# A streaming encoder layer on one core: a VectorE copy, one idle product, later loads of the mix's weights, and unequal last parts

## The chip, the cores and the metric

The kernel runs on one core of one Trainium2 chip. The metric is the device time of one execution in microseconds (us).

## The reference, cut to what matters

One layer works on 2176 tokens (2048 of a prompt, and 8 streams with 16 tokens each) of 1024 features. A projection feeds two groups of heads: a gated unit whose rows are mixed over 128 tokens by a triangular matrix, and a band attention. The two halves go through an output projection, and a layer norm closes.

```python
h = jnp.einsum('bsd,de->bse', x, w_in)
v_a = _layernorm(jax.nn.gelu(h[..., o[1]:o[2]]), ln_v_g, ln_v_b)
mix = jnp.einsum('gts,bnsgc->bntgc', jnp.tril(w_s), vc) + b_s.T[...]      # a = u * mix
y = jnp.concatenate([a_out * silu(z_a), b_out * silu(z_b)], axis=-1)
out = jnp.einsum('bse,ed->bsd', y, w_out)
return _layernorm(ALPHA * x + out, g, bb)
```

For the streams the mix uses the first 16 rows and columns of `w_s` only.

## The kernel before, in words

Every large product is done in three products of a shortened format: each operand is split into a high part (ScalarE copies it into that format) and a low part (VectorE subtracts the high part from the original), and TensorE adds high x high, high x low and low x high. Work is written out by hand for five engines, each with its own list of instructions in program order; semaphores tie them together. SP's list holds most DMAs, ScalarE's list the loads of weights.

**The opening.** The 2176 tokens are 17 tiles of 128. The first stage ("va") projects each tile on 512 columns, v_a's. Its weights come as 8 pieces (`wp`, order `KO`), and each tile's transposed x comes as two halves of 4 blocks. ScalarE asks for the 8 pieces (L1143 to L1148), then turns piece 0, the first half of tiles 0 and 1, pieces 1 and 2, the second halves of tiles 0 and 1, and the other pieces into high parts (L1149 to L1158), each counted in `w_high` or `xt_high`. VectorE makes the low parts in the same order (L1480 to L1490, counted in `w_ready` and `xt_ready`). TensorE first runs `IDLE_PRODUCTS` products of a tile of ones that nobody reads (L1882 to L1884), then takes tiles 0 and 1 together, piece by piece: high of tile 0, high of tile 1, two products with the weights' low part, two with x's low part (L1886 to L1903). The first product of the fifth piece counts in `xt_freed`, which lets SP reload tile 0's first half for tile 2.

From tile 2 on (L1904) TensorE goes: first half of tile t, the mix of tile t - 2, second half of tile t. The mix of tile 0 waits for `const_ready` at 6 (L1831), which is the two masks that GpSimd puts on the mix's weights: `wt` for the prompt and `wts`, the eight 16 x 16 blocks for the streams (L940 to L943). It begins with products that sum the rows of `wt`. Behind the masks in GpSimd's list stands, for each tile, the sum that turns a tile's mean and variance into a scale and a shift (L988 to L997); ScalarE then normalises the tile (L1102) and only then turns the second half of tile t + 2 (L1170 to L1180). The mix of tile 1 waits for its offsets `mix_b`, which VectorE makes once, in tile 1's turn, behind the low part of tile 3's second half (L1523 to L1531), from the row sums, `b_sgu` (`bs`) and the columns `v_cols`.

**SP's list in the opening** (L741 to L756): the four halves of tiles 0 and 1; `bs`; `v_cols`; `wt`; eight loads of blocks into `wts` behind the wait for `zeroed` (GpSimd's clearing of it); `rel_in`, the table of relative biases; then for each tile t the two halves of tile t + 2, each behind the wait that its buffer is free (`load_xt`, L631 to L639), and at t = 1, 4, 7, 10 four loads of x for the next stage.

**The end.** The last stage projects each tile's 1024 output columns in two halves. For the last four tiles VectorE does the layer norm by itself (`finish`, L1697 to L1710): subtract the mean and multiply by the gain, in two parts of 512 columns, wait for GpSimd's inverse deviation, multiply by it and add the offset, in two parts again. SP stores tiles 15 and 16 part by part (L912 to L916).

```python
            for t in range(TILES):
                for h in range(2):
                    if t + 2 < TILES:
                        load_xt("va", t + 2, h)
                    if h == 0 and t in X_LOADS:
                        load_xo(X_LOADS.index(t))
```

Of the kernel before, what the change touches and what calls it, by code (L numbers as in the profile page):

```python
# [6 lines left out]
P = 128  # L7
D = 1024
KC = D // P
HK = KC // 2  # L10
# [3 lines left out]
TILES = T // P  # L14
# [14 lines left out]
MASKED = 3.0e38  # L29
KR = 6  # L30
TAIL = 4
IDLE_PRODUCTS = 10

# [21 lines left out]
KO = [0, 1, 2, 3, 4, 5, 7, 6]  # L57
# [124 lines left out]
BUILT = builds()  # L182
# [42 lines left out]
XT_ORDER = [("va", 0, 0), ("va", 1, 0), ("va", 0, 1), ("va", 1, 1)]  # L225
XT_ORDER += [(*e, h) for e in XT_TILES[2:] for h in range(2)]
XT_COUNT = {half: n + 1 for n, half in enumerate(XT_ORDER)}


def xt_place(kind, t, h):  # L230

    if (kind, t) == ("v", TILES - 1):
        return 6 + h
    if t % 2:
        return 2 + h
    return 4 + h if kind == "v" and t > V_SPLIT else h


def xt_signal(kind, t):

    return 2 if (kind, t) == ("v", TILES - 1) else t % 2
# [44 lines left out]
V_CYCLES = TILES - V_EARLY  # L286
CYCLES = V_CYCLES + 2 * TILES
START = [V_CYCLES + 2 * n for n in range(TILES)]
STORE = [START[n] + (3 if n < TILES - TAIL else 2) for n in range(TILES)]
X_LOAD = [V_CYCLES, V_CYCLES] + [STORE[n - 2] for n in range(2, TILES)]  # L290
POOL_TILES = TILES - TAIL
# [40 lines left out]
def hybrid_stream_step(nc, x, x_t, x_tiles, w_tok, w_pair, w_o, w_sgu, b_sgu, ln_v_g, ln_v_b, ln_v_cols, rel_rev, ln_g, ln_b,  # L332
# [6 lines left out]
    with ctx:  # L339
# [3 lines left out]
        def sem(name):  # L343
            return ctx.enter_context(nc.semaphore(name))
# [13 lines left out]
        def at(name, offset, shape, dt=f32):  # L358
# [10 lines left out]
        lnvg, lnvb, bs, wt, wts = (at(name, x_slot * j + 8 * HK * WIDTH[0], shape) for j, (name, shape) in enumerate((  # L369
            ("lnvg", [512]), ("lnvb", [512]), ("bs", [GRP, P]), ("wt", [GRP, P]), ("wts", [GRP, P]))))  # L370
# [31 lines left out]
        xt_h = [at(f"xt_h{b}", a, [HK, P], f32r) for b, a in enumerate(xt_at)]  # L402
        xt_l = [at(f"xt_l{b}", a + 2048, [HK, P], f32r) for b, a in enumerate(xt_at)]
        xt_f = [at(f"xt_f{b}", a + 2048, [HK, P]) for b, a in enumerate(xt_at)]
# [9 lines left out]
        v_cols = at("v_cols", here + 224, [2 * GRP])  # L414
# [64 lines left out]
        cols_loaded = sem("cols_loaded")  # L479
# [10 lines left out]
        xt_loaded = [[sem(f"xt_loaded{b}_{h}") for h in range(2)] for b in range(3)]  # L490
        q_part = sem("q_part")
        q_copied = sem("q_copied")
        xt_high = sem("xt_high")
        xt_ready = sem("xt_ready")
        xt_freed = sem("xt_freed")
# [134 lines left out]
        def _(sp):  # L630
# [109 lines left out]

            for t, h in ((0, 0), (1, 0), (0, 1), (1, 1)):  # L741
                load_xt("va", t, h)
            sp.dma_start(bs[:].rearrange("p g t -> p (g t)"), b_sgu.partition_broadcast(P)).then_inc(cols_loaded, 16)
            sp.dma_start(v_cols[:], ln_v_cols).then_inc(cols_loaded, 16)
            sp.dma_start(wt[:], w_sgu).then_inc(par_loaded, 16)
            sp.wait_ge(zeroed, 1)
            for b in range(SB):
                sp.dma_start(wts[b * SN:(b + 1) * SN, :, b * SN:(b + 1) * SN],
                             w_sgu[0:SN, :, 0:SN]).then_inc(blocks_loaded, 16)
            sp.dma_start(rel_in[0:HEADS, :], rel_rev).then_inc(rel_loaded, 16)  # L750
            for t in range(TILES):
                for h in range(2):
                    if t + 2 < TILES:
                        load_xt("va", t + 2, h)
                    if h == 0 and t in X_LOADS:
                        load_xo(X_LOADS.index(t))  # L756
                if t == 4:
                    sp.wait_ge(rel_shifted, 2)
                    sp.wait_ge(rel_filled, 1)
                    flat = REL - (2 * CLIP + 1)  # L760
                    sp.dma_start(s_rel[:, 0:flat], rel[0:HEADS, 0:flat]).then_inc(rel_stored, 16)
                    sp.dma_start(s_rel[:, flat:REL], rel_in[0:HEADS, :]).then_inc(rel_stored, 16)
                if t == 11:
                    sp.dma_start(lnvg[:], ln_v_g.partition_broadcast(P)).then_inc(lnv_loaded, 16)
                    sp.dma_start(lnvb[:], ln_v_b.partition_broadcast(P)).then_inc(lnv_loaded, 16)
                if t >= 3:
                    store_mix(t - 3)
                if t == 13:
                    for last in (6, 7):
                        s, stored = STAGED["va", last][0]  # L770
                        sp.wait_ge(st_stored[s], 16 * (stored + 1))
                    load_mixb(0)
                    load_mixb(1)
# [137 lines left out]

            for n in range(TILES - 2, TILES):  # L912
                for part in range(2):
                    at_d = slice(D // 2 * part, D // 2 * (part + 1))
                    sp.wait_ge(last_ready, 2 * (n - POOL_TILES) + part + 1)
                    sp.dma_start(y_out[n * P:n * P + P, at_d], r[n % 2][:, at_d]).then_inc(r_stored[n % 2], 16)  # L916
            for s in range(2):
# [131 lines left out]
        def _(act):  # L1049
# [25 lines left out]
            def xt_high_part(kind, t, h):  # L1075
                b = xt_place(kind, t, h)
                act.wait_ge(xt_loaded[xt_signal(kind, t)][h], 16 * (xt_loads_before(kind, t) + 1))
                nc.scalar.activation(xt_h[b][:], xt_f[b][:], ACT.Copy).then_inc(xt_high, 1)
# [68 lines left out]
            for j in KO[2:]:  # L1147
                load_piece(0, j)  # L1148
            w_high_part(("piece", 0, KO[0]))  # L1149
            for t in range(2):  # L1150
                xt_high_part("va", t, 0)
            for j in KO[1:3]:
                w_high_part(("piece", 0, j))
            for t in range(2):
# [217 lines left out]
        def _(dve):  # L1372
            def w_low_part(what):
                dve.wait_ge(w_high, BUILT[what])
                if what[0] == "piece":
                    j = what[2]
                    nc.vector.tensor_tensor(wp[:, j, 1, :], wp_raw[:, j, 1, :], wp[:, j, 0, :].bitcast(f32),
                                            ALU.subtract).then_inc(w_ready, 1)
                else:
                    p = what[2]  # L1380
                    nc.vector.tensor_tensor(wf[:, p, 1], operand[p][:], wf[:, p, 0].bitcast(f32),  # L1381
                                            ALU.subtract).then_inc(w_ready, 1)
# [16 lines left out]

            def xt_low_part(kind, t, h):  # L1400
                b = xt_place(kind, t, h)
                dve.wait_ge(xt_high, XT_COUNT[kind, t, h])
                nc.vector.tensor_tensor(xt_l[b][:], xt_f[b][:], xt_h[b][:].bitcast(f32),
                                        ALU.subtract).then_inc(xt_ready, 1)

# [72 lines left out]
                                                   op0=ALU.mult, op1=ALU.subtract).then_inc(finished, 1)  # L1478

            nc.vector.memset(st[3][:, 0:P], 1.0).then_inc(warm_ready, 1)  # L1480
            w_low_part(("piece", 0, KO[0]))
            for t in range(2):
                xt_low_part("va", t, 0)
# [213 lines left out]
            def finish(n):  # L1697

                dve.wait_ge(ln_loaded, 32)
                dve.wait_ge(mv_ready, n + 1)  # L1700
                for part in range(2):
                    at_d = slice(D // 2 * part, D // 2 * (part + 1))
                    nc.vector.scalar_tensor_tensor(out=r[n % 2][:, at_d], in0=r[n % 2][:, at_d], scalar=mv[n % 2][:, 0:1],
                                                   in1=gain[:, at_d], op0=ALU.subtract, op1=ALU.mult).then_inc(last_centred, 1)
                dve.wait_ge(rstd_ready, n + 1)
                for part in range(2):
                    at_d = slice(D // 2 * part, D // 2 * (part + 1))
                    dve.wait_ge(last_centred, 2 * (n - POOL_TILES) + part + 1)
                    nc.vector.scalar_tensor_tensor(out=r[n % 2][:, at_d], in0=r[n % 2][:, at_d], scalar=rstd[n % 2][:],
                                                   in1=offset[:, at_d], op0=ALU.mult, op1=ALU.add).then_inc(last_ready, 1)  # L1710
# [63 lines left out]
        def _(pe):  # L1774
# [111 lines left out]
            for i, kc in enumerate(KO):  # L1886
                h, j = i // HK, kc % HK
                pe.wait_ge(w_high, BUILT["piece", 0, kc])
                for t in range(2):
                    if i % HK == 0:  # L1890
                        pe.wait_ge(xt_high, XT_COUNT["va", t, h])
                    made = nc.tensor.matmul(tile_ps[t], xt_h[xt_place("va", t, h)][:, j, :], wp[:, kc, 0, :], start=i == 0, stop=False)  # L1892
                    if i == HK:
                        made.then_inc(xt_freed, 1)
                pe.wait_ge(w_ready, BUILT["piece", 0, kc])
                for t in range(2):
                    nc.tensor.matmul(tile_ps[t], xt_h[xt_place("va", t, h)][:, j, :], wp[:, kc, 1, :], start=False, stop=False)
                if i % HK == 0:
                    pe.wait_ge(xt_ready, XT_COUNT["va", 1, h])
                for t in range(2):  # L1900
                    made = nc.tensor.matmul(tile_ps[t], xt_l[xt_place("va", t, h)][:, j, :], wp[:, kc, 0, :], start=False, stop=i == KC - 1)
                    if i == KC - 1:
                        made.then_inc(proj_done, 1)  # L1903
# [247 lines left out]
```

## Time and profile before

| What | us |
|---|---|
| median of three runs | 1004.79 (1003.35 to 1004.91) |
| profiled execution | 1004.2 |
| its span, first to last instruction | 1002.4 |
| TensorE busy in the span | 993.2 |
| VectorE, ScalarE, GpSimd busy | 671.6, 507.6, 178.3 |

The span is what the trace shows; the profiled execution's own time is 1.8 us longer. Engines in the rows: PE is TensorE (PEld its loading of weights), DVE VectorE, ACT ScalarE, POOL GpSimd, SPq and ACTq the lists that issue DMAs. A timeline row is a start, a length from the first to the last of a run of equal instructions, engine, line of the kernel, operation, operands and count; in brackets stands how long the engine was idle before it and what ended that. A line can be that of a helper that serves many tiles.

### The profile page before, as it was taken

Reading aid. Unit: us, or ns where it says so; the run is one execution under the profiler, and the core shown is the slowest. Engines: PE = TensorE matmul, PEld = TensorE weight load, DVE = VectorE, ACT = ScalarE, POOL = GpSimd, SP = SyncE. Lnnn points to the kernel's source line nnn. Section 1 sums busy time; section 2 is a strip of 40 time slices with the busy share of each in tenths; the row PEclk is TensorE's granted clock in tenths of the full one; section 3 lists DMA queues with packets and bytes.
Section 4 is the critical chain, followed back from the end, with each engine's and each line's share of the span. In section 5 each row is a group of like instructions: output and inputs, shape, how many; then the busy total and the mean of one; then the engine's idle time right before and its main releaser. Section 6 shows DMA issues by size and latency. Waiting matters only on the chain.

```text
span 1002.4 us, 19281 instructions
## 1 busy us (share of the span) xinstructions
PE 993.2 (99%) x7464; PEld 860.4 (86%) x7464; DVE 671.6 (67%) x1334; ACT 507.6 (51%) x994; POOL 178.3 (18%) x181
## 2 busy tenths in 40 slices
PE   9999999999999999999999999999999999999997
PEld 7888888888888899999999987778888888888885
DVE  4776877656657776465556525977777777776765
ACT  5455644344444553334343426766666666666630
POOL 1557521000001010200000000022222222222200
PEclk9999999999999999999999999999999999999998
DMA  6556354365756423335554486763434433333212
GB/s 217 175 169 217 110 163 128 109 183 169 204 161 233 145 88 102 89 118 156 154 147 128 148 277 224 257 240 142 139 139 140 139 140 128 117 131 124 95 64 84
DMA packets 122858, 152.65 MB, mean 152 GB/s; under 512 B 13176, under 2 KB 75792, under 8 KB 122768
## 3 DMA queue, kind: packets, MB, share of 16 engines
q1 hardware_dynamic: 107792, 124.16, 38.5%
q10 hardware_dynamic: 14976, 27.27, 8.6%
q8 instruction: 59, 0.97, 0.4%
q14 instruction: 31, 0.25, 0.1%
HBM read 106.29 MB, written 48.26 MB: 154 GB/s over the span
## 4 chain that ended last, share of the span: by engine, by line
PE 99%; ACTq 0%; DVE 0%; ACT 0%; issue 0%; DVEq 0%
PE s_ps L1877 24%; PE oo_ps L2066 18%; PE pt_ps L1877 12%; PE s_ps L1788 9%; PE oo_ps L2028 7%; PE oo_ps L1877 6%; PE s_ps L1957 6%; PE s_ps L1806 4%; PE pt_ps L1999 3%; PE pt_ps L1788 2%; PE s_ps L2066 2%; PE oo_ps L1806 2%; PE oo_ps L1842 2%; PE s_ps L1986 1%; PE pt_ps L1806 1%; PE s_ps L1892 1%
## 5 line engine op out<-in xcount | busy, mean ns | idle before, releaser
L1877 PE MATMUL s_ps<-xo_h,wf 128*128 128x288 f32 (+1 forms) x960 | 232.6, 327 | 0.0
L1877 PEld LDWEIGHTS s_ps<-xo_h,wf 128*128 128x128 f32 x960 | 163.7, 188 | 12.5 <-issue 0.2
L1877 PE MATMUL s_ps<-xo_l,wf 128*128 128x288 f32 (+1 forms) x480 | 156.7, 326 | 0.0
L1620 DVE CUSTOM_DVE_ANT_1 prob<-s_ps,bias 128x640 f32<-128x640 f32 (+1 forms) x112 | 85.8, 803 | 59.9 <-PE s_ps L1957 59.9
L1274 ACT ACTIVATE prob<-prob,low 128x640 f32<-128x640 f32 (+3 forms) x128 | 97.5, 763 | 46.1 <-DVE low L1620 46.0
L1877 PE MATMUL pt_ps<-xo_h,wf 128*128 128x288 f32 (+1 forms) x480 | 119.5, 327 | 0.0
L2066 PE MATMUL oo_ps<-wo_h,yh 128*128 128x512 f32 x248 | 100.6, 406 | 0.0
L2066 PE MATMUL oo_ps<-wo_l,yh 128*128 128x512 f32 x248 | 97.0, 391 | 0.0
L2066 PE MATMUL oo_ps<-wo_h,yl 128*128 128x512 f32 x248 | 97.0, 391 | 0.0
L1877 PEld LDWEIGHTS s_ps<-xo_l,wf 128*128 128x128 f32 x480 | 90.1, 188 | 6.2
L1877 PEld LDWEIGHTS pt_ps<-xo_h,wf 128*128 128x128 f32 x480 | 82.4, 188 | 6.2
L1381 DVE TENSOR_TENSOR wf<-a,wf 128x512 fp32r<-128x512 f32 x80 | 56.0, 702 | 45.5 <-ACT wf L1073 45.5
L1115 ACT ACTIVATE copy<-s_ps 128x512 f32<-128x512 f32 (+1 forms) x60 | 37.4, 624 | 90.8 <-PE s_ps L1877 89.1
L1644 DVE TENSOR_SCALAR prob<-prob,rden 128x640 f32<-128x640 f32 (+4 forms) x128 | 79.5, 621 | 4.6
L1788 PE MATMUL s_ps<-wp,xt_h 128*128 128x512 f32 x256 | 80.8, 397 | 0.0
L1877 PE MATMUL pt_ps<-xo_l,wf 128*128 128x288 f32 (+1 forms) x240 | 78.3, 326 | 0.0
L1381 DVE TENSOR_TENSOR wf<-s,wf 128x512 fp32r<-128x512 f32 x60 | 43.5, 726 | 51.5 <-ACT wf L1073 50.8
L1073 ACT ACTIVATE wf<-a 128x512 fp32r<-128x512 f32 x80 | 49.5, 623 | 39.2 <-DVE s L1398 15.9
L1266 ACT ACTIVATE pt<-pt_ps 128x1024 f32<-128x1024 f32 (+3 forms) x64 | 60.4, 944 | 16.4 <-PE pt_ps L1999 14.1
L2028 PE MATMUL oo_ps<-pt,v 128*64 128x128 f32 x1120 | 68.4, 276 | 0.0
L1957 PE MATMUL s_ps<-k,q 64*128 64x256 f32 (+3 forms) x696 | 67.3, 323 | 0.1
L2028 PEld LDWEIGHTS oo_ps<-pt,v 128*64 128x64 f32 x1120 | 60.4, 137 | 6.1 <-issue 3.0
(192 smaller groups left out, 1910.9 us busy)
## 6 DMA issues: line engine op xcount, KB each, us to landing
a<-w_pair ACTq DMA_DIRECT2D x80, 256.0 KB, 3.1
xt_f<-x_tiles SPq DMA_DIRECT2D x44, 256.0 KB, 3.0
r<-x SPq DMA_DIRECT2D x17, 512.0 KB, 3.6
s_k<-st SPq DMA_DIRECT2D x32, 256.0 KB, 2.9
s_q<-st SPq DMA_DIRECT2D x32, 256.0 KB, 2.8
q<-s_q SPq DMA_DIRECT2D x16, 512.0 KB, 4.1
k<-s_k SPq DMA_DIRECT2D x16, 512.0 KB, 6.0
y_out<-r SPq DMA_DIRECT2D x15, 512.0 KB, 2.6
```

Of the source, the lines that this page charges most:

```text
L1073: nc.scalar.activation(wf[:, p, 0], operand[p][:], ACT.Copy).then_inc(w_high, 1)
L1266: nc.scalar.activation(held, pt_both[:, :, 0:m, :], ACT.Copy).then_inc(pt_copied, 1)
L1274: nc.scalar.activation(prob[s][:, 0:n], prob[s][:, 0:n], ACT.Exp, bias=low[:, s:s + 1], scale=-1.0, accum_out=den[:, s:s + 1]).then_inc(ex ...
L1381: nc.vector.tensor_tensor(wf[:, p, 1], operand[p][:], wf[:, p, 0].bitcast(f32), ALU.subtract).then_inc(w_ready, 1)
L1620: nc.vector.tensor_tensor_reduce(out=out, in0=src, in1=b, scale=1.0, scalar=MASKED, op0=ALU.add, op1=ALU.min, accum_out=low[:, s:s + 1]).t ...
L1644: nc.vector.tensor_scalar(prob[s][:, lo:n], prob[s][:, lo:n], rden[:, s:s + 1], None, ALU.mult).then_inc(normed, 1)
L1788: made = nc.tensor.matmul(out, xx[b][:, kc % HK, :], wp[:, kc, side, :], start=(h, i, a) == (0, 0, 0), stop=(h, i, a) == (1, HK - 1, 2))
L1806: made = nc.tensor.matmul(v_ps[t], xx[pas][p][:, kc % HK, at_t], wp[:, kc, side, :], start=start and (i, a) == (0, 0), stop=stop and (i, a ...
L1877: made = nc.tensor.matmul(out, wf[:, p, side, kc, :], xx[pas][p][:, kc, c * n:(c + 1) * n], start=kc == 0 and a == 0 and p in (0, 1, 3, 5) ...
L1957: last = nc.tensor.matmul(s_ps[h][:, at_c:at_c + count * P], q[t % 2][rows, a * GRP + p, :], key_slots(rows, c * GRP + p, first, count), s ...
L2028: last = nc.tensor.matmul(o_ps[64 * h:64 * h + 64, p * P:(p + 1) * P], v[(t + 1 - nk + b) % KR][:, p * P + 64 * h:p * P + 64 * h + 64], pt ...
L2066: last = nc.tensor.matmul(out_bank(half), y[n % 2][:, c, :], w[h][:, c, :], start=c == 0 and a == 0, stop=c == KC - 1 and a == 2)
```

## The change

VectorE copies the first half of tile 0 into the short format, under a semaphore of its own, in place of ScalarE. One idle product is added. `xt_low_part` and the products of tiles 0 and 1 now count ScalarE's high parts without that one (`XT_HIGH`), and TensorE waits for each tile's low part by itself. In SP's list the loads of `wt`, `wts`, `bs` and `v_cols` come behind a wait for ScalarE's fourth piece, and the load of tile 2's first half comes between `wt` and `wts`. At the end the two parts are 640 and 384 columns in place of 512 and 512.

```diff
-IDLE_PRODUCTS = 10
+IDLE_PRODUCTS = 11
+XT_HIGH = {half: n for n, half in enumerate(XT_ORDER)}
+LAST_PARTS = [(0, 640), (640, 1024)]
...
             for t, h in ((0, 0), (1, 0), (0, 1), (1, 1)):
                 load_xt("va", t, h)
-            sp.dma_start(bs[:].rearrange("p g t -> p (g t)"), b_sgu.partition_broadcast(P)).then_inc(cols_loaded, 16)
-            sp.dma_start(v_cols[:], ln_v_cols).then_inc(cols_loaded, 16)
+            sp.wait_ge(w_high, BUILT["piece", 0, KO[3]])
             sp.dma_start(wt[:], w_sgu).then_inc(par_loaded, 16)
+            load_xt("va", 2, 0)
             sp.wait_ge(zeroed, 1)
             for b in range(SB):
                 sp.dma_start(wts[b * SN:(b + 1) * SN, :, b * SN:(b + 1) * SN],
                              w_sgu[0:SN, :, 0:SN]).then_inc(blocks_loaded, 16)
+            sp.dma_start(bs[:].rearrange("p g t -> p (g t)"), b_sgu.partition_broadcast(P)).then_inc(cols_loaded, 16)
+            sp.dma_start(v_cols[:], ln_v_cols).then_inc(cols_loaded, 16)
             sp.dma_start(rel_in[0:HEADS, :], rel_rev).then_inc(rel_loaded, 16)
             for t in range(TILES):
                 for h in range(2):
-                    if t + 2 < TILES:
+                    if t + 2 < TILES and (t or h):
                         load_xt("va", t + 2, h)
...
-                    at_d = slice(D // 2 * part, D // 2 * (part + 1))
+                    at_d = slice(*LAST_PARTS[part])
...
             w_high_part(("piece", 0, KO[0]))
-            for t in range(2):
-                xt_high_part("va", t, 0)
+            xt_high_part("va", 1, 0)
...
-                dve.wait_ge(xt_high, XT_COUNT[kind, t, h])
+                if (kind, t, h) == ("va", 0, 0):
+                    dve.wait_ge(first_high, 1)
+                else:
+                    dve.wait_ge(xt_high, XT_HIGH[kind, t, h])
...
             nc.vector.memset(st[3][:, 0:P], 1.0).then_inc(warm_ready, 1)
+            b = xt_place("va", 0, 0)
+            dve.wait_ge(xt_loaded[xt_signal("va", 0)][0], 16)
+            nc.vector.tensor_copy(xt_h[b][:], xt_f[b][:]).then_inc(first_high, 1)
             w_low_part(("piece", 0, KO[0]))
...
                 for t in range(2):
-                    if i % HK == 0:
-                        pe.wait_ge(xt_high, XT_COUNT["va", t, h])
+                    if i == 0 and t == 0:
+                        pe.wait_ge(first_high, 1)
+                    elif i % HK == 0:
+                        pe.wait_ge(xt_high, XT_HIGH["va", t, h])
...
-                if i % HK == 0:
-                    pe.wait_ge(xt_ready, XT_COUNT["va", 1, h])
                 for t in range(2):
+                    if i % HK == 0:
+                        pe.wait_ge(xt_ready, XT_COUNT["va", t, h])
```

`LAST_PARTS` is used in `finish` (both loops) and in SP's last stores.

## Rows read from the trace of the kernel before

**Rows 1.** The page, part 1 (busy time) and part 4 (chain that ended last).
```profile
PE 993.2 (99%) x7464; PEld 860.4 (86%) x7464; DVE 671.6 (67%) x1334; ACT 507.6 (51%) x994; POOL 178.3 (18%) x181
...
PE 99%; ACTq 0%; DVE 0%; ACT 0%; issue 0%; DVEq 0%
```

**Rows 2.** Chain in order of time, opening: start us, us, what.
```profile
8.71 0.85 PE s_ps L1901 x2
...
10.42 0.66 PE s_ps L1897 x2
11.08 0.45 PE s_ps L1901 x2
...
19.24 0.45 PE s_ps L1901 x2
...
30.20 0.06 issue
```

**Rows 3.** One stretch of the opening: busy time by engine, granted clock, DMA share.
```profile
9.50:10.00 0.50, 0.50 (x3) 0.40 (x2) 0.50 (x2) 0.45 (x2) 0.00 (x0) 1.00 1.04 364
```

**Rows 4.** Timeline of the opening, PE, ACT and DVE: start us, us, engine, line.
```profile
1.10 4.64 PE L1884 MATMUL oo_ps<-st 128*128 128x128 f32 x20 [1.10 <-DVE st L1480]
...
6.39 1.47 PE L1892 MATMUL s_ps<-wp,xt_h 128*128 128x512 f32 x2 [0.65 <-ACT xt_h L1078]
...
6.38 0.63 ACT L1078 ACTIVATE xt_h<-xt_f 128x512 fp32r<-128x512 f32 x1
...
10.47 0.63 ACT L1060 ACTIVATE wp<-wp_raw 128x512 fp32r<-128x512 f32 x1
...
14.29 0.63 ACT L1060 ACTIVATE wp<-wp_raw 128x512 fp32r<-128x512 f32 x1 [0.16 <-DMA wp_raw<-w_tok]
...
5.75 0.69 DVE L1377 TENSOR_TENSOR wp<-wp_raw,wp 128x512 fp32r<-128x512 f32 x1 [4.71 <-ACT wp L1060]
...
11.13 0.69 DVE L1377 TENSOR_TENSOR wp<-wp_raw,wp 128x512 fp32r<-128x512 f32 x1
```

**Rows 5.** Timeline of SP's queue, the loads of the opening: issue and its length.
```profile
2.65 0.51 SPq L743 DMA_DIRECT2D bs<-b_sgu  x1
...
7.23 2.51 SPq L748 DMA_DIRECT2D wts<-w_sgu  x4
...
9.78 0.53 SPq L750 DMA_DIRECT2D rel_in<-rel_rev  x1
14.51 5.79 SPq L638 DMA_DIRECT2D xt_f<-x_tiles  x3
...
19.49 0.80 SPq L638 DMA_DIRECT2D xt_f<-x_tiles  x2
...
22.24 0.43 SPq L638 DMA_DIRECT2D xt_f<-x_tiles  x1
```

**Rows 6.** Loads: us to landing (14 to 20 us); issue ns min/median/max by tile.
```profile
xt_f<-x_tiles SPq DMA_DIRECT2D x3, 256.0 KB, 2.5
...
L907 SPq DMA_DIRECT2D sbias<-s_skew x8: 419/420/1528, 644.6 to 649.0; - x8
...
L638 SPq DMA_DIRECT2D xt_f<-x_tiles x13: 327/366/432, 0.8 to 38.0; - x13
```

**Rows 7.** Timeline, POOL, ACT and DVE from 15 to 30 us.
```profile
15.33 0.81 POOL L942 TENSOR_SCALAR_AFFINE_SELECT wts<-wts 128x512 f32<-128x512 f32 x1 [0.88 <-DMA wts<-w_sgu]
...
21.12 0.19 POOL L992 TENSOR_TENSOR rstd_v<-mv_v,eps 128x1 f32<-128x1 f32 x1 [4.99 <-DVE mv_v L1516]
...
22.35 0.81 ACT L1102 ACTIVATE st<-st,shift_v,rstd_v 128x512 f32<-128x512 f32 x1 [2.25 <-POOL shift_v L996]
...
28.98 1.12 DVE L1529 SCALAR_TENSOR_TENSOR mix_b<-oo_ps,v_cols,bs 128x128 f32<-128x128 f32 x4
```

**Rows 8.** The end: VectorE's last pair; DMA rate from 999 to 1003 (40 slices).
```profile
998.48 1.41 DVE L1709 SCALAR_TENSOR_TENSOR r<-r,rstd_o,offset 128x512 f32<-128x512 f32 x2
...
GB/s 0 0 0 0 0 0 0 0 0 0 82 348 348 389 369 348 430 369 369 369 369 410 451 348 226 21 0 0 0 0 0 0 0 0 0 0 0 0 0 0
```

More of the change, by code:

```diff
@@ L492, in hybrid_stream_step @@
         q_copied = sem("q_copied")
+        first_high = sem("first_high")
         xt_high = sem("xt_high")
@@ L1701, in finish @@
                 for part in range(2):
-                    at_d = slice(D // 2 * part, D // 2 * (part + 1))
+                    at_d = slice(*LAST_PARTS[part])
                     nc.vector.scalar_tensor_tensor(out=r[n % 2][:, at_d], in0=r[n % 2][:, at_d], scalar=mv[n % 2][:, 0:1],
@@ L1706, in finish @@
                 for part in range(2):
-                    at_d = slice(D // 2 * part, D // 2 * (part + 1))
+                    at_d = slice(*LAST_PARTS[part])
                     dve.wait_ge(last_centred, 2 * (n - POOL_TILES) + part + 1)
```

## The prediction

> **What bounds the kernel now.** I read the page first: TensorE is busy 99% of the span, and the chain that ended last is TensorE for 99% [rows 1]. So a change can only move the time where TensorE waits or runs slowly: at the opening and after the last product. The chain in order of time shows the opening [rows 2]: two products take 0.85 us until 10.4 us and 0.45 us from 11.08 on. For 512 columns each that is 1.2 GHz and then 2.4 GHz. The granted-clock column reads 1.00 already at 9.5 us [rows 3]; the spacing of the products contradicts it, and I go by the spacing. Before the rise TensorE had run its idle products from 1.10 to 5.74, had stood still for 0.65 us, and had then worked on [rows 4]. Tiles 0 and 1 end at 19.69. From there the chain is dense: tile 2 with its mix, tile 3's first half, and at 30.20 only 0.06 us of waiting before the mix of tile 1 [rows 2]. Whatever reaches that point late makes the whole kernel late, since nothing after it waits.
>
> The sum is made against the profiled execution, 1004.2 us: a span of 1002.4 and 1.8 around it. That is 0.6 under the median of the runs shown (1004.79) and inside them (1003.35 to 1004.91). A measurement of this kernel can tell about 0.2% from no change, 2.0 us here.
>
> **Part 1: VectorE makes the first high half, one idle product more.** Ten idle products take 4.64 us, so an eleventh takes 0.46 and ends at about 6.2. The first real product, which waited for ScalarE until 6.39, can start there: the copy needs x's half, which ScalarE turned before 6.38, and VectorE idles 4.71 us until 5.75 [rows 4]. No row has this copy; between nothing and the 0.69 of VectorE's subtraction of the same 128x512 it is hidden, and I take 0.69, the nearest in shape. If the half came after 5, VectorE's first low part would slip from 5.75, and its products, behind the second one, have about 1 us of slack. But the second product needs tile 1's half, which ScalarE turns from 6.38 to 7.01, behind its transfer and not behind the instruction that is taken away. So the second product stays just behind 7.01 and the path gains 0. What changes is the rest: the 0.65 us before the first real product becomes at most as much between the first and the second, and what little TensorE waited between those two before goes into it.
>
> **Part 2: what an earlier clock would be worth.** Only ScalarE and VectorE set the pace then. ScalarE makes the fourth piece's high part from 10.47 to 11.10 (behind two x halves, so not sooner), VectorE its low part from 11.13 to 11.82 [rows 4]. The last four products of that piece follow at 0.23 each: 12.75. Four pieces of six products at 0.23 end at 18.2, with the later pieces in time even at their present dates (the last high part, at 14.29, is needed after 16.8). The 0.23 is half of the 0.45 of a pair [rows 2]. Against 19.69 that is 1.5 us, the most this can give; without an earlier rise it gives 0.
>
> **Part 3: the loads asked for later.** This part costs. The queue order becomes: wait for the fourth high part (11.10), the mix's weights, tile 2's first half (which waits for the first product of the fifth piece), eight small block loads, bias, columns, table, and only then tile 2's second half. Taking these from before the rise lets the weight pieces land sooner, which by part 2 nobody on the path waits for.
> - Late side (clock as before): tile 2's first half leaves at 14.51 as now [rows 5]. Behind it come its own 0.4, eight block loads of 0.64 (four take 2.51 with their gaps: 5.1), and three loads of about 0.54 with the gap (1.6). Tile 2's second half leaves at 21.6 instead of 19.49: 2.1 late. Tile 3's second half, 2.75 behind it in the same queue, leaves at 24.4 instead of 22.24, also 2.1 late.
> - Early side: the fifth piece starts at 12.75, its product ends some 0.4 later, so that half leaves at 13.2, tile 2's second half at 20.3 and tile 3's second half at 23.0: 0.8 late, although TensorE is 1.5 early.
> - GpSimd sits in the same trap: it stands at the mask of the blocks before it can turn tile 0's statistics into a scale and a shift. Now it masks at 15.33 and starts tile 0's at 21.12 [rows 7]. The eighth block load would leave at 18.1 (early) or 19.4 (late). No row has it alone; a load from a fairly free queue lands in 2.5 [rows 6], so the mask (0.81) ends at 21.4 or 22.7. Normalisation, 22.35 now, starts at 22.6 or 23.9, and tile 2's second half is multiplied 0.2 or 1.5 us later than now.
> - The later of the two counts. Tile 3's second half goes through ScalarE and VectorE right up to the mix's offsets at 28.98 [rows 7], whose first four end at 30.1, just where TensorE comes to the mix of tile 1 at 30.25. That mix is then 0.8 (early) or 2.1 (late) behind. The two delays are not added, being in one chain.
> What I cannot price is whether 0.64 was a price of the crowded queue. The other end: later loads into 16 partitions issue in 0.42 [rows 6]. I take 0.64, because these are the same instructions, and the last four still cost that after ScalarE had stopped issuing. Bias and columns at 20 us are needed at 28.98 and have cover; if that went, the same offsets would wait.
>
> **Part 4: the end.** The two instructions of 512 columns start 0.66 apart (998.48, 1.41 together [rows 8]); 640 and 384 columns sum to the same, so VectorE ends at 999.9 as now. The first store leaves later by a quarter of 0.66, about 0.15, and is larger. The DMA engines move data without a break from 1000.0 to 1001.5 (slices of 0.1 us [rows 8]), so a start that is 0.15 later can end 0.15 later; at best the last store's missing 64 KB (at about 380 GB/s) gives 0.17. I take +0.1, the transfers being back to back. For tile 15 the same split lies beside products.
>
> **The sum.** Early clock: 1004.2 + 0.8 + 0.1 = 1005.1. Late clock: 1004.2 + 2.1 + 0.1 = 1006.4.
>
> **Which of the two, and the rivals.**
> - **Forecast, 1005.1 (chance 0.42):** the fuller opening brings the rise before 8 us, and the later loads eat it and 0.8 more. For it: in the trace the clock did not rise behind the idle products, a pause followed them, and it rose once work had run without one. Against: a pause of 0.6 is still there.
> - **Slower, 1006.4 and up (0.32):** the rise stays where it was, since the unbroken work still begins behind 7.01. Then the block loads are pure loss of 2.1. Each us that the rise comes later costs another 0.47 (0.85 against 0.45 for two products), so from a rise at about 11.5 on the time is over 1006.8; I give that 0.2. The runs shown differ by 1.56 us, about what an early rise is worth, so the place of the rise may differ from run to run.
> - **Issue is cheap in an empty queue, 1003.5 (0.14):** eight loads at 0.46 with the gap instead of 0.64 give back 1.4 us, so with an early clock tile 2's second half leaves at 18.9 and the mix of tile 1 is 0.6 to 0.8 early; 1004.2 - 0.8 + 0.1. With 0.33 an issue, the shortest x load [rows 6], 1003.0.
> - **The change does nothing (0.07):** late clock and cheap issue, 1004.4. The remaining 0.05 is for what no row shows.
> The Trainium skill ("TensorE: Matmul & The Clock Gate", Part 1) says that the monitor behind the clock runs free and does not start anew with the kernel, so that the same kernel sees the rise at different points. By that rule one idle product shifts only the odds, and either of the first two rows above can be seen in single runs; the trace, being one execution, neither confirms nor denies it.
>
> **How the numbers follow.** The forecast is the likeliest case, 1005.1. The range goes from the cheap issue with an early clock, 1002.9, to a late clock with a rise 1.3 us after the present one, 1007.0. Faster than 1002.8 needs cheap issue at its lowest end and a gain at the end: 0.06. Slower than 1006.8 is two thirds of the slower rival and some unknowns: 0.24. The rest, 0.70, is within 0.2%.
>
> **What would show it.** In the changed profile: pairs of 0.45 us from about 8 us on (forecast) or 0.85 until after 10 (rival); the eight block loads between 13 and 20 us at 0.6 each; GpSimd's second mask at 20 or later, its wait ended by those loads; tile 2's second half leaving after 20; TensorE idle before the mixes of tiles 0 and 1, together up to 2 us; the first product near 6.0 and the second still near 7.06. I am wrong if the block loads take 0.4 each, if the mask is done before tile 0's statistics are, or if the second product comes sooner.

## The result and the profile after

The changed kernel takes 1006.41 us (median of ten executions, 1005.95 to 1008.67); beside it the kernel before took 1004.34 (ten executions, 1003.28 to 1005.01). The ratio is 1.0025, with an interval of 1.0016 to 1.0033. By the medians it is 2.1 us slower, inside the forecast's range and 1.3 over its 1005.1. The interval lies on both sides of the 0.2% line and its middle on the slower side, which had 0.24. The profiled execution took 1006.41, with a span of 1004.4; before it was 1004.2 and 1002.4, so the span has 2.0 of the difference. Executions of one kernel differ by 1.7 to 2.7 us here and by up to 4 in the runs below, in the profiles mostly with the place where TensorE's clock rises or falls, so medians alone don't show where a few tenths went. The ratios below leave out three executions of the kernel before that took 1219 us and more.

The page of the kernel after, parts 1 and 4, against [rows 1]:

```profile
PE 992.6 (99%) x7466; PEld 859.0 (86%) x7466; DVE 670.5 (67%) x1335; ACT 507.3 (51%) x993; POOL 177.8 (18%) x181
...
PE 96%; DMA 1%; SPq 1%; DVE 1%; issue 0%; ACT 0%; POOLq 0%; ACTq 0%; DVEq 0%; POOL 0%
```

The engines do the same work. The chain that ended last is TensorE for 96% and no longer for 99: some 30 us of it now go through SP's list, a transfer and VectorE. The timelines of TensorE and VectorE in the opening of the kernel after (start us, length us, engine, line, operation; in brackets the idle time before and what ended it), against [rows 2, 4]:

```profile
1.10 5.06 PE L1895 MATMUL oo_ps<-st 128*128 128x128 f32 x22 [1.10 <-DVE st L1488]
5.82 0.80 PE L1905 MATMUL s_ps<-wp,xt_h 128*128 128x512 f32 x1
7.01 0.50 PE L1905 MATMUL s_ps<-wp,xt_h 128*128 128x512 f32 x1 [0.40 <-ACT xt_h L1084]
7.34 0.62 PE L1910 MATMUL s_ps<-wp,xt_h 128*128 128x512 f32 x2
7.81 0.62 PE L1914 MATMUL s_ps<-wp,xt_l 128*128 128x512 f32 x2
...
18.38 0.61 PE L1799 MATMUL s_ps<-wp,xt_h 128*128 128x512 f32 x2
...
22.99 1.16 PE L1853 MATMUL oo_ps<-wt,st 128*128 128x128 f32 x8 [0.51 <-ACT st L1108]
...
24.80 0.72 PE L1799 MATMUL s_ps<-wp,xt_h 128*128 128x512 f32 x2 [0.65 <-DVE xt_l L1411]
...
32.11 1.13 PE L1853 MATMUL oo_ps<-wt,st 128*128 128x128 f32 x8 [1.60 <-DVE mix_b L1540]
...
4.46 0.43 DVE L1491 CAST xt_h<-xt_f 128x512 fp32r<-128x512 f32 x1 [3.42 <-DMA xt_f<-x_tiles]
...
30.84 1.12 DVE L1540 SCALAR_TENSOR_TENSOR mix_b<-oo_ps,v_cols,bs 128x128 f32<-128x128 f32 x4
```

The same two places in the kernel before, the start of tile 2 and the mix of tile 1:

```profile
19.53 0.62 PE L1788 MATMUL s_ps<-wp,xt_h 128*128 128x512 f32 x2
...
30.25 1.13 PE L1842 MATMUL oo_ps<-wt,st 128*128 128x128 f32 x8
```

The copy hides in VectorE's idle time, and the first product starts at 5.82 in place of 6.39. The second still starts at 7.01, when ScalarE has turned tile 1's half. From 7.34 pairs start 0.46 or 0.47 apart: the clock is at 2.4 GHz from the second product on, where before it rose between 10.4 and 11.1. Tile 2 starts at 18.38 in place of 19.53. So far TensorE is 1.15 us early. Then it waits: 0.51 for ScalarE's normalisation in the mix of tile 0, 0.65 before tile 2's second half, 1.60 before the mix of tile 1. That mix starts at 32.11, behind `mix_b` at 30.84, where [rows 7] have 28.98: 1.86 later. The lists that lead there, SP, ScalarE and GpSimd of the kernel after, against [rows 5, 7]:

```profile
13.35 0.33 SPq L642 DMA_DIRECT2D xt_f<-x_tiles  x1
13.72 5.18 SPq L752 DMA_DIRECT2D wts<-w_sgu  x8
18.95 0.58 SPq L754 DMA_DIRECT2D bs<-b_sgu  x1
19.57 0.43 SPq L755 DMA_DIRECT2D v_cols<-ln_v_cols  x1
20.05 0.37 SPq L756 DMA_DIRECT2D rel_in<-rel_rev  x1
20.46 0.82 SPq L642 DMA_DIRECT2D xt_f<-x_tiles  x2
21.33 1.85 SPq L648 DMA_DIRECT2D xo_f<-x_t  x4
23.23 4.92 SPq L642 DMA_DIRECT2D xt_f<-x_tiles  x3
...
22.13 0.81 ACT L1108 ACTIVATE st<-st,shift_v,rstd_v 128x512 f32<-128x512 f32 x1 [3.18 <-POOL shift_v L1002]
...
29.57 0.63 ACT L1084 ACTIVATE xt_h<-xt_f 128x512 fp32r<-128x512 f32 x1 [1.52 <-DMA xt_f<-x_tiles]
...
20.30 0.64 POOL L948 TENSOR_SCALAR_AFFINE_SELECT wts<-wts 128x512 f32<-128x512 f32 x1 [5.54 <-DMA wts<-w_sgu]
```

Eight block loads of 4 KB hold SP for 5.18 us. Tile 2's second half leaves at 20.46 in place of 19.49, tile 3's second half at 23.23 in place of 22.24: 1.0 late. ScalarE gets it at 29.57, 6.3 us after it left. The kernel before has the same load from 22.24 on, 5.4 us to landing. First the row of the loads of the kernel before, then that of the chain of waits of the kernel after:

```profile
xt_f<-x_tiles SPq DMA_DIRECT2D x1, 256.0 KB, 5.4
...
23.23 6.32 DMA xt_f<-x_tiles
```

So the half is late twice: 1.0 in leaving, 0.9 on the way.

Nothing after the mix of tile 1 changed: from its start to the end of the span are 972.1 us before (30.25 to 1002.4) and 972.3 after (32.11 to 1004.4). The rest is the end of the kernel, in the timeline of VectorE of the kernel after, against [rows 8]:

```profile
1000.34 1.41 DVE L1720 SCALAR_TENSOR_TENSOR r<-r,rstd_o,offset 128x640 f32<-128x640 f32 x2
```

VectorE's last pair still takes 1.41; from its start to the end of the span are 4.06 us (1000.34 to 1004.4), where they were 3.92 (998.48 to 1002.4). The spans are given to 0.1 us, so this difference alone is 0.1 to 0.2. Together 1.86 and 0.14 make the 2.0 of the span.

### The profile page after: what moved, and what is told of

It is laid out like the page before. It is cut to its first block, busy times and chain, and to the rows that moved or that the text cites. A ratio compares the mean times of both kernels' runs of the same rounds, so it can differ in the third digit from the quotient of the medians.

```text
span 1004.4 us, 19285 instructions
## 1 busy us (share of the span) xinstructions
PE 992.6 (99%) x7466; PEld 859.0 (86%) x7466; DVE 670.5 (67%) x1335; ACT 507.3 (51%) x993; POOL 177.8 (18%) x181
## 4 chain that ended last, share of the span: by engine, by line
PE 96%; DMA 1%; SPq 1%; DVE 1%; issue 0%; ACT 0%; POOLq 0%; ACTq 0%; DVEq 0%; POOL 0%
PE s_ps L1888 24%; PE oo_ps L2079 18%; PE pt_ps L1888 12%; PE s_ps L1799 8%; PE oo_ps L2041 7%; PE oo_ps L1888 6%; PE s_ps L1970 6%; PE s_ps L1817 4%; PE pt_ps L2012 3%; PE pt_ps L1799 2%; PE s_ps L2079 2%; PE oo_ps L1817 2%; PE oo_ps L1853 1%; PE s_ps L1999 1%; PE pt_ps L1817 1%; DMA wp_raw<-w_tok 1%
```

## The experiments

My theory after the result: all of the loss is tile 3's second half, late in part through the block loads' issue and in part because the bias (256 KB) and the columns go through the queue just ahead of it. Rivals: the clock rose late as the second row of the prediction had it; the split of the end costs more than 0.1; or the new opening itself costs time. Ratios are to the kernel before on the same chip, beside each run.

**The loads put back**, and nothing else of the change:

```diff
-            sp.wait_ge(w_high, BUILT["piece", 0, KO[3]])
+            sp.dma_start(bs[:].rearrange("p g t -> p (g t)"), b_sgu.partition_broadcast(P)).then_inc(cols_loaded, 16)
+            sp.dma_start(v_cols[:], ln_v_cols).then_inc(cols_loaded, 16)
...
-            load_xt("va", 2, 0)
...
-                    if t + 2 < TILES and (t or h):
+                    if t + 2 < TILES:
```

> The change with SP's list as it was before (part 3 undone), all else kept. Executions fall into two groups by where the clock rises: before at about 1003.3 and 1004.9, changed kernel at about 1006.3 and 1008.6. Queue theory (the whole loss is the order of the loads): 1003.4 in the group with the early rise and 1005.0 in the other (0.15 for the end), and more executions in the early group than the kernel before has, so a median near 1003.5. Rival (VectorE's copy, the split waits or the idle product cost it): it stays at 1006.

1003.53 us (1003.16 to 1005.25), ratio 0.9999 [0.999, 1.0008]. The chain of waits of this run, in order of time, is TensorE alone up to the mix of tile 1:

```profile
26.38 2.72 PE pt_ps L1797 x12
29.10 1.06 PE oo_ps L1851 x8
```

The mix starts without a wait, 3 us before that of the kernel after (32.11). With the old order of loads the whole loss is gone; the opening and the end together cost nothing that the times can show. Both profiles have the early clock, so the new order of loads costs 3.1 us of the path. The kernel before's profile has the late clock, and its mix starts at 30.25; the comparison with it shows only 1.86 of that.

**The new order of loads alone**, in the kernel before: the edit above the other way round.

> The kernel before with the new order of SP's loads alone. Queue theory: 1006.1 with the early rise, 1008.4 with the late one (the changed kernel less 0.15 for the end), TensorE idle about 1.6 us before the mix of tile 1. Rival (copy, waits, idle product): as before, 1003.3 and 1004.9.

1006.73 us (1006.06 to 1008.85, 5 executions), ratio 1.0033 [1.002, 1.0045]. So the order of the loads is enough for the loss. The expectation had 1008.4 for a late clock; the profiled execution has one and took 1006.73, so a late clock alone does not explain the slower group, two of five here. The clock of this execution, by stretches of 1 us (the busy time of the engines, then the granted clock, the DMA share and GB/s), and the rows of SP and TensorE:

```profile
6.00:7.00 1.00, 0.47 (x1) 0.19 (x1) 1.00 (x2) 0.83 (x2) 0.00 (x0) 1.00 1.06 385
...
8.00:9.00 1.00, 1.00 (x3) 0.78 (x3) 0.69 (x1) 0.38 (x1) 0.00 (x0) 0.50 1.01 373
...
11.00:12.00 1.00, 1.00 (x6) 0.77 (x6) 1.00 (x3) 1.00 (x4) 0.00 (x0) 1.00 0.40 152
```

```profile
14.84 5.18 SPq L748 DMA_DIRECT2D wts<-w_sgu  x8
...
24.37 4.77 SPq L638 DMA_DIRECT2D xt_f<-x_tiles  x3
...
32.88 1.13 PE L1844 MATMUL oo_ps<-wt,st 128*128 128x128 f32 x8 [1.38 <-DVE mix_b L1531]
```

This is the prediction's late side: pairs at 1.2 GHz until about 11, and tile 3's second half leaves at 24.37 (24.4 in the prediction). But the chain of waits gives its way to ScalarE 5.95 us, and the mix of tile 1 is 2.6 behind 30.25, not 2.1. The late side was undersized in the same place as the early one, by 0.5.

**The blocks early, the rest as in the change**: the eight loads go to the front of the list, and bias, columns and table stay behind tile 2's first half.

```diff
-            sp.wait_ge(w_high, BUILT["piece", 0, KO[3]])
-            sp.dma_start(wt[:], w_sgu).then_inc(par_loaded, 16)
-            load_xt("va", 2, 0)
             sp.wait_ge(zeroed, 1)
             for b in range(SB):
...
+            sp.wait_ge(w_high, BUILT["piece", 0, KO[3]])
+            sp.dma_start(wt[:], w_sgu).then_inc(par_loaded, 16)
+            load_xt("va", 2, 0)
```

> The changed kernel with the eight block loads back at the front (behind the four x halves); the wait, the mix's weights, tile 2's first half, bias, columns and table follow. Queue theory: the queue is then free when tiles 0 and 1 end, so 1003.4 early and 1005 late, as with the old order. If it is the 256 KB of the bias behind the wait that cost, and not the block loads' issue: no better than 1005.4 early.

1003.55 us (1003.05 to 1005.56), ratio 0.9998 [0.999, 1.0007]; the mix of tile 1 starts at 29.32. Without the 5.18 us of issue, bias and columns leave at 13.8, long before the x halves, and nothing is lost that the times can show.

**The bias and columns early, the blocks as in the change:**

```diff
+            sp.dma_start(bs[:].rearrange("p g t -> p (g t)"), b_sgu.partition_broadcast(P)).then_inc(cols_loaded, 16)
+            sp.dma_start(v_cols[:], ln_v_cols).then_inc(cols_loaded, 16)
             sp.wait_ge(w_high, BUILT["piece", 0, KO[3]])
...
-            sp.dma_start(bs[:].rearrange("p g t -> p (g t)"), b_sgu.partition_broadcast(P)).then_inc(cols_loaded, 16)
-            sp.dma_start(v_cols[:], ln_v_cols).then_inc(cols_loaded, 16)
```

> The changed kernel with bias and columns at the front and only the block loads late. Two shares of the loss are told apart: the block loads (5.2 us of issue and GpSimd's mask) and the bias with its 256 KB ahead of tile 3's second half. Queue theory: tile 3's second half leaves at 22.2 and lands in about 5.4, the mix of tile 1 starts at 30.2 to 30.4 in place of 32.1, so 1004.4 early and 1006.6 late. If the block loads alone make the loss, it stays at 1006.3; if the bias alone, 1003.4.

1004.24 us (1003.91 to 1005.77), ratio 1.0005 [0.9997, 1.0014], where the whole change has 1.0025. **The bias late, the blocks early** is the other half of this pair: the blocks go to the front as two runs above, and bias, columns and table go right ahead of tile 2's second half, where the change has them, and are kept there by a wait. This is the part that brings them there:

```diff
+                    if (t, h) == (0, 1):
+                        sp.wait_ge(proj_done, DONE["va", 0])
+                        sp.dma_start(bs[:].rearrange("p g t -> p (g t)"), b_sgu.partition_broadcast(P)).then_inc(cols_loaded, 16)
+                        sp.dma_start(v_cols[:], ln_v_cols).then_inc(cols_loaded, 16)
+                        sp.dma_start(rel_in[0:HEADS, :], rel_rev).then_inc(rel_loaded, 16)
```

> The changed kernel with the block loads at the front, and bias, columns and table late, right ahead of tile 2's second half (behind the end of tile 0's products): the bias share of the loss by itself. Queue theory: three issues of 0.6, 0.43 and 0.37 delay tile 3's second half by 1.5 us, and the bias's 256 KB before it in the queue by another 0.7 to 0.9, so the mix of tile 1 starts near 31.5 (29.3 with the loads early), 1005.5 early and 1007 late. If only the block loads cost: 1003.5. GpSimd's mask is out of it: its two masks end before 15.

1005.46 us (1004.96 to 1007.40), ratio 1.0014 [1.0005, 1.0023]. Rows of the two, first the bias early (SP, GpSimd, ScalarE, TensorE), then the bias late (SP, ScalarE, TensorE):

```profile
22.31 11.81 SPq L642 DMA_DIRECT2D xt_f<-x_tiles  x5
...
20.28 0.63 POOL L948 TENSOR_SCALAR_AFFINE_SELECT wts<-wts 128x512 f32<-128x512 f32 x1 [5.77 <-DMA wts<-w_sgu]
...
27.35 0.63 ACT L1084 ACTIVATE xt_h<-xt_f 128x512 fp32r<-128x512 f32 x1
...
29.89 1.13 PE L1853 MATMUL oo_ps<-wt,st 128*128 128x128 f32 x8
```

```profile
22.44 11.66 SPq L642 DMA_DIRECT2D xt_f<-x_tiles  x4
...
28.99 0.63 ACT L1086 ACTIVATE xt_h<-xt_f 128x512 fp32r<-128x512 f32 x1 [1.81 <-DMA xt_f<-x_tiles]
...
31.53 1.78 PE L1855 MATMUL oo_ps<-wt,st 128*128 128x128 f32 x8 [1.89 <-DVE mix_b L1542]
```

In this pair tile 3's second half leaves at 22.31 and at 22.44, 0.13 apart. With the bias early ScalarE does not wait for it and turns it at 27.35; with bias and columns ahead in the queue it waits 1.81 and turns it at 28.99, 1.64 later, and the mix of tile 1 starts 1.64 later too. So bias and columns cost transfer time there, not only their issue. (The medians, from two chips, differ by 1.2, the ratios by 0.9 us.) The pair differs in the place of the blocks too. The blocks early and the bias late differ in bias, columns and table alone. Their chains of waits have the half, first the blocks early, then the bias late:

```profile
21.23 5.53 DMA xt_f<-x_tiles
...
22.44 6.53 DMA xt_f<-x_tiles
```

That is 1.2 us later in leaving and 1.0 longer on the way, and the mix of tile 1 starts 2.2 later (29.32 and 31.53). The way varies between runs: in the ten traces with bias and columns early and the four loads of x just ahead it takes 4.7 to 5.5 us, in the three with bias and columns just ahead as well 5.9 to 6.5. No run separates the 256 KB of bias from the 4 KB of columns. With the bias early what is left of the loss is GpSimd's chain: the mask waits until 20.28 for the blocks, tile 2's second half is multiplied late, and the mix starts at 29.89 where the first run had 29.03.

**The opening, part by part**, with the old order of loads and equal ends. The idle product alone, in the kernel before:

```diff
-IDLE_PRODUCTS = 10
+IDLE_PRODUCTS = 11
```

> The kernel before with 11 idle products in place of 10, nothing else. So far executions with the early rise (the faster of two groups, 1003.3 against 1004.7) are 20 of 37 with the old opening and 35 of 43 with the copy on VectorE and 11 idle products (26 of 32 of them in kernels of this study). If the idle product alone shifts the odds: 8 in 10 in the fast group, median near 1003.4. If it takes both, or the copy: 5 or 6 in 10, a median anywhere between the groups. If the place of the rise is chance that no edit here moves: also 5 or 6 in 10.

1003.45 us (1002.96 to 1004.66), ratio 0.9993 [0.9984, 1.0001]. The copy and the split waits with ten idle products (the kernel after with the loads put back as above, and):

```diff
-IDLE_PRODUCTS = 11
+IDLE_PRODUCTS = 10
-LAST_PARTS = [(0, 640), (640, 1024)]
+LAST_PARTS = [(0, 512), (512, 1024)]
```

> The changed kernel with the old order of loads, equal last parts and 10 idle products: VectorE's copy and the split waits alone. If the copy alone shifts the odds (a first product at 5.8 in place of 6.4): 8 in 10 in the fast group, median near 1003.4. If it takes the idle product too: 5 or 6 in 10. The level of the fast group stays at 1003.3 either way, since the second product still starts at 7.0.

1003.74 us (1003.05 to 1006.36), ratio 0.9999 [0.999, 1.0008]. Both together, the same edit without its first two lines:

> The changed kernel with the old order of loads and equal last parts: copy on VectorE and 11 idle products remain. 8 in 10 executions in the fast group at 1003.3, median 1003.3; at the end 7.15 us again. If the copy or the idle product cost something beside the odds, the fast group lies above that of the kernel before.

1003.39 us (1003.17 to 1005.14), ratio 0.9996 [0.9987, 1.0004]. Thirteen idle products in that kernel:

```diff
-IDLE_PRODUCTS = 11
+IDLE_PRODUCTS = 13
```

> The changed kernel with the old order of loads and equal last parts, and 13 idle products: they end at about 7.0, when tile 1's half is turned, so that TensorE hardly pauses between them and the work. If the pause decides where the clock rises, or whether it falls again: nearly every execution in the fast group at 1003.3 and none over 1004.5. If the rise is chance that idle products don't move: 8 of 11 or fewer, as with 11 idle products.

1003.88 us (1003.46 to 1004.41), ratio 0.9999 [0.999, 1.0008]. None of the four is measurably faster or slower. An eleventh idle product may change how often the clock is high early: 8 of 11 executions of the opening alone and 9 of 11 with the idle product alone were below 1004 us, and 14 of 32 of the kernel before beside them. That is not shown: the copy alone, with ten idle products, has 7 of 11, which can be told from neither, and the clock was read in one execution of each kernel only. (In this study the seven profiled executions below 1004 us all had the early clock.) With thirteen none was above 1004.5, but the best were no better, and all lay above the expected 1003.3. The profiled execution with thirteen began the mix of tile 1 at 29.73 and lost 0.7 more where a band's product waited once for VectorE. In the profile of the opening alone (1005.14) the early clock was lost again. Its timeline of TensorE and stretches of 1 us:

```profile
5.80 0.50 PE L1903 MATMUL s_ps<-wp,xt_h 128*128 128x512 f32 x1 [0.39 <-ACT wp L1064]
7.92 0.80 PE L1903 MATMUL s_ps<-wp,xt_h 128*128 128x512 f32 x1 [1.61 <-ACT xt_h L1082]
8.51 1.05 PE L1908 MATMUL s_ps<-wp,xt_h 128*128 128x512 f32 x2
```

```profile
5.00:6.00 1.00, 0.61 (x5) 0.40 (x3) 0.38 (x2) 0.63 (x1) 0.00 (x0) 1.00 0.91 217
...
9.00:10.00 1.00, 1.00 (x4) 0.81 (x3) 0.42 (x2) 0.90 (x2) 0.00 (x0) 0.50 1.06 395
...
12.00:13.00 1.00, 1.00 (x6) 0.80 (x5) 0.93 (x2) 0.75 (x2) 0.00 (x0) 1.00 1.01 307
```

The first product takes 0.50, at 2.4 GHz. Tile 1's half came late in this execution, TensorE stood for 1.61, and the products that follow run at 1.2 GHz until after 11. That is the 0.65 of [rows 4], moved behind the first product; Part 1 gave it 0.65 at most, and a late transfer made more of it here.

**The unequal ends alone**, in the kernel before (the lower pair of lines in SP's last stores and in both loops of `finish`):

```diff
+LAST_PARTS = [(0, 640), (640, 1024)]
-                    at_d = slice(D // 2 * part, D // 2 * (part + 1))
+                    at_d = slice(*LAST_PARTS[part])
```

> The kernel before with last parts of 640 and 384 columns alone. From the end of the last product's group to the end of the span the kernel before takes 7.15 us (VectorE's last residual to the last instruction), the changed one 7.30. Forecast's theory: 7.30 here too, since the larger first store begins later and the second stands behind it. Rival (the 0.15 is scatter or belongs to the opening): 7.15. The time itself is within its scatter of before.

1004.48 us (1003.13 to 1007.08), ratio 1.0001 [0.9992, 1.001]. The profile fell on the slowest execution, with pairs of 0.85 until 13.5; the end can be read all the same. VectorE's last pair starts at 1000.99 and the span ends at 1005.0: 4.01 us, 0.1 more than before as near as the rounded span shows. The fourteen traces settle it: from the start of TensorE's last product to the end of the span they have 7.57 to 7.59 us with equal parts and 7.72 to 7.74 with 640 and 384 columns. So the unequal parts cost 0.15, as forecast to 0.05.

**A kernel that might beat both.** Thirteen idle products, the blocks at the front, equal ends, and the fourth piece's high and low parts ahead of the second halves of tiles 0 and 1:

```diff
-            for j in KO[1:3]:
+            for j in KO[1:4]:
...
-            for j in KO[3:]:
+            for j in KO[4:]:
```

> As the one with 13 idle products, and the block loads at the front with the rest of the order of the changed kernel, and on ScalarE and VectorE the fourth piece's parts ahead of the second halves of tiles 0 and 1. With the early rise TensorE waits about 0.3 us for the fourth piece's low part at 11.9; here that part is made by 11.4. Expected 0.3 to 0.4 us under the fast group, 1003.0, nearly every execution there. If that wait is not on the path: 1003.3.

1003.65 us (1003.14 to 1004.47), ratio 0.9999 [0.999, 1.0008]. The expected 1003.0 was missed. The mix of tile 1 started at 29.61, behind a wait of 0.61 for `mix_b`, and the chain of waits went through the four loads of x for the next stage (20.0 to 21.8) and tile 3's second half (21.85, 5.20 long). So in the next run those four go behind that half:

```diff
-                    if h == 0 and t in X_LOADS:
+                    if h == 1 and t in X_LOADS:
```

> The kernel of e11_fourth_first with the four xo loads put behind the second half of the same tile of x in SP's queue, not ahead of it. If the next bound is tile 3's second half, which left at 21.85 us behind those four loads: it leaves some 1.9 us earlier, lands before 26, and the mix of tile 1 starts about 28.9 in place of 29.61 with no wait ahead of it, so about 1003.0. If that load was not the bound, or if the residual path that the four loads feed comes late instead: 1003.6 as e11_fourth_first, or above.

1003.42 us (1002.74 to 1006.85), ratio 1.0 [0.9991, 1.0009]. Timelines of SP and TensorE:

```profile
18.16 2.27 SPq L642 DMA_DIRECT2D xt_f<-x_tiles  x3
20.48 1.86 SPq L648 DMA_DIRECT2D xo_f<-x_t  x4
...
28.80 1.13 PE L1853 MATMUL oo_ps<-wt,st 128*128 128x128 f32 x8
```

All three x halves leave before 20.5, and the mix of tile 1 starts at 28.80 with no wait. The mechanism was as expected, and the profiled execution, at 1002.74, is the fastest of its eleven. But the faster half of the kernel before's executions beside it lay at 1002.9 to 1003.8 already, and the median gains nothing that can be told from no change. No kernel of the study is measurably faster than the kernel before.

Side by side, the start of the mix of tile 1, the span of the profiled execution, and the difference of the two:

| kernel | mix of tile 1, us | span, us | rest, us |
|---|---|---|---|
| before | 30.25 | 1002.4 | 972.1 |
| after | 32.11 | 1004.4 | 972.3 |
| loads back | 29.03 | 1001.3 | 972.3 |
| loads only | 32.88 | 1005.0 | 972.1 |
| blocks early | 29.32 | 1001.6 | 972.3 |
| bias early | 29.89 | 1002.0 | 972.1 |
| bias late | 31.53 | 1005.3 | 973.8 |
| idle product alone | 29.27 | 1001.4 | 972.1 |
| copy alone | 29.27 | 1001.5 | 972.2 |
| opening alone | 30.91 | 1003.2 | 972.3 |
| thirteen idle products | 29.73 | 1002.7 | 973.0 |
| ends alone | 31.86 | 1005.0 | 973.1 |
| fourth piece first | 29.61 | 1001.9 | 972.3 |
| x halves first | 28.80 | 1001.0 | 972.2 |

Eleven of the fourteen differ at one point, which is what the prediction had said of it: whatever reaches it late makes the kernel late. In three the rest is longer: by 1.6 with the bias late (the last section tells why), by 0.8 with thirteen idle products and by 1.0 with the ends alone, where TensorE waited later on, 0.7 for VectorE in the one and 0.4 for ScalarE in the other. What made up the rest of the 1.0 was not looked for.

## Why the prediction was right, and where its size was off

**What bounds the kernel** held: TensorE is dense after the mix of tile 1, and the table gives that rest as 972.1 to 972.3 us in eleven of fourteen profiles.

**Part 1** was right. The path gains 0: the second product starts at 7.01, as forecast. The copy takes 0.43, not the 0.69 taken from the subtraction, and is hidden in either case. The Trainium skill ("VectorE: DVE Perf Modes", "The perf-mode tier table") says that an operation with one tensor operand may run at a higher rate in fp32 than one with two; the trace agrees, with 0.43 against 0.69 for the same 128x512.

**Part 2** was right. The early clock came in the profiled execution, and tile 2 starts 1.15 us sooner (18.38 for 19.53), of the 1.5 at most. That it came is in part luck: the kernel before, too, has executions below 1004 us, 14 of 32, and no run shows that the change brought the early clock.

**Part 3** had the right mechanism, and its steps on SP's list hold to 0.2 us: eight block loads 5.18 (5.1), tile 2's second half at 20.46 (20.3), tile 3's second half at 23.23 (23.0). GpSimd's mask and the normalisation came 0.5 sooner than said. The term that was mis-sized is tile 3's second half: it "leaves at 24.4 instead of 22.24, also 2.1 late", with "tile 3's second half at 23.0: 0.8 late" on the early side. It took the delay in leaving for the delay in arriving. The early side measured 1.86 in place of 0.8, of which 1.0 is leaving and 0.9 the way (6.3 us in place of 5.4). The bias had been priced as one more issue of 0.54; bias and columns travel in the same queue just ahead of the x halves, and the runs show what that is worth on the way: 1.0 us between the blocks early and the bias late, 1.5 between the bias early and late (5.0 and 6.5 us), where the half leaves at the same time. The late side was off in the same way: 24.37 as said, but 2.6 in place of 2.1.

**Issue is cheap in an empty queue** is ruled out: 0.60 and a gap of 0.04 for each block load, the crowded queue's price. The Trainium skill ("DMA: Bandwidth & Descriptors", "Issuing engines are not separate DMA queues") says that the time to start a transfer is usually small beside the transfer. For these loads of 4 KB it is not small here: each takes 0.60 us of SP's list and lands some 2.0 us after it was asked for. Eight of them take 5.18 us, twice the 2.5 us in which a 256 KB half lands in a fairly free queue [rows 6].

**Part 4** was right: 0.15 in all the traces with 640 and 384 columns, against +0.1.

**The slower rival** gave 1006.4, the very median, but for a reason that the profile excludes: it had the clock rise late, and here it rose early. That its number came out is chance: the early clock's gain (1.15 us) and the longer way (0.9), neither of which it had, nearly cancel. With a late clock the loads alone give 1006.7. The forecast's sum, with the measured 1.86 and 0.14 in place of 0.8 and 0.1, gives 1004.2 + 1.86 + 0.14 = 1006.2, against the 1006.41 of the profiled execution (which has 2.0 around its span, not 1.8).

## What to carry to other kernels

Here loads that were moved ahead of another in one queue cost that one twice: their time of issue, and time on the way. So add up both up to the load that the path waits for, and look at when the data lands, not when it is asked for. Small loads can hold the issuing list longer than large ones (0.60 us for each 4 KB block here, 0.33 for a 256 KB half; why was not tested), and belong where that list has nothing urgent behind it. Where a kernel is dense after one point, the start of that point plus a constant gives the span of most variants, here to 0.2 us in eleven of fourteen, while whole executions of one kernel differ by 1.5 and more. Check the rest of the trace all the same: three had lost 0.8 to 1.6 us later.

## What the runs showed of the hardware that was not expected

The clock can rise under the idle products, fall again behind a pause and rise once more. In the loads-only run the first two products take 0.47 and 0.50 us, the clock column reads 1.00 at 6 us, 0.50 from 8 to 10 and 1.00 from 11; in the opening alone the first product runs at 2.4 GHz, and after a pause of 1.61 the next ones run at 1.2. The kernel after has a pause of 1.60 before the mix of tile 1 and keeps 1.00 behind it; the run with the bias late has one of 1.89 at the same place and loses the clock. Its stretches of 1 us:

```profile
31.00:32.00 1.00, 0.47 (x3) 0.50 (x4) 1.00 (x5) 0.00 (x0) 0.00 (x0) 0.91 0.00 0
32.00:33.00 1.00, 1.00 (x8) 1.00 (x6) 1.00 (x3) 0.00 (x0) 0.00 (x0) 0.50 0.00 0
...
35.00:36.00 1.00, 1.00 (x6) 0.77 (x5) 0.00 (x0) 0.98 (x2) 0.00 (x0) 0.88 0.65 225
```

That is the 1.6 us by which this execution's rest is longer in the table. So a wait in the opening can have a second price, here of some 1.6 us in one profiled execution. The column by itself is no proof: in the run with the ends alone it reads 1.00 from 7 to 13 us while pairs start 0.85 apart. Whether the kernel after's executions at 1008.5 and above are of this kind was not shown, none of them having been profiled.
